# Block two's high weights meet both parts of the activations in one 512-column product, with the halves added outside TensorE

## What is computed

```python
h = concatenate([meta, x])                                   # 272 tokens
hn = rms_norm(h, norm_mix_g)
u, gb_in, gc_in, v_in, ga_lin, gbr_lin = split(hn @ w_in)     # each 2048 wide
pooled = causal_multiscale_pool(u)                            # windows 2, 4, 8, 16, minus the token
y_a = einsum("blgc,gcd->blgd", pooled, pool_w) * pool_scale   # 4 groups of 512
y_b = (gb_in * causal_conv3(gc_in * v_in, conv_w)) @ conv_out_w
g_a, g_b = split(sigmoid(concatenate([ga_lin, gbr_lin]) + b_gate))
h = h + (g_a * y_a + g_b * y_b) @ w_o
hn = rms_norm(h, norm_ffn_g)
gate, up = split(hn @ w_gate_up)                              # 5632 wide each
h = h + (silu(gate) * up) @ w_down
out = rms_norm(h, norm_final_g)[:, N_META:]
```

## Time and profile before

| | us |
|---|---|
| three runs, median (lowest to highest) | 3471.76 (3467.4 to 3475.43) |
| the profiled execution: its own time | 3463.28 |
| its span, first to last instruction | 3462.0 |
| PE busy, PEld busy | 3311.9, 2870.4 |
| DVE busy, ACT busy, POOL busy | 1650.5, 1359.4, 172.5 |
| mean granted TensorE clock | 0.982 of 2.4 GHz |

### The profile page before, as it was taken

One profiled execution on the slowest core, in us unless ns is written; L12 is line 12 of the kernel. 1 busy time (PEld: TensorE's weight loads), 2 busy tenths in 40 slices (PEclk: granted clock), 3 DMA queues, 4 the chain that ended last, 5 costly groups with the idle time before them and its releaser, 6 DMA issues.

```text
span 3462.0 us, 52180 instructions
## 1 busy us (share of the span) xinstructions
PE 3311.9 (96%) x21982; PEld 2870.4 (83%) x21982; DVE 1650.5 (48%) x2678; ACT 1359.4 (39%) x2179; POOL 172.5 (5%) x252
## 2 busy tenths in 40 slices
PE   6799999988999989999799999999999999999998
PEld 1488888863458888887459999999999999999998
DVE  0422233374563363355575675555555645545444
ACT  1422232344442263333454443344444444444343
POOL 2000000001001101000101000000000000000000
PEclk9999999998999999999899999999999999999999
DMA  9533222226744254443436455555555555555554
GB/s 344 187 122 122 91 93 96 84 74 239 251 174 151 92 193 142 140 134 108 156 119 200 151 182 177 182 178 189 186 186 188 165 186 187 189 186 186 189 185 138
DMA packets 154314, 566.06 MB, mean 164 GB/s; under 512 B 17472, under 2 KB 19648, under 8 KB 152928
## 3 DMA queue, kind: packets, MB, share of 16 engines
q1 hardware_dynamic: 147648, 529.52, 45.7%
q0 software_dynamic: 6432, 33.20, 2.7%
HBM read 550.07 MB, written 12.58 MB: 163 GB/s over the span
## 4 chain that ended last, share of the span: by engine, by line
PE 88%; DMA 5%; DVE 3%; ACT 2%; issue 1%; POOL 0%; SPq 0%; DVEq 0%; ACTq 0%; POOLq 0%
PE ps L695 20%; PE ps L696 20%; PE ps L697 20%; PE ps L688 7%; PE ps L690 7%; PE ps L689 7%; DMA sb_raw<-in_stream 5%; PE ps L614 2%; PE ps L816 1%; PE ps L802 1%; PE ps L779 1%; PE ps L795 1%; PE ps L770 1%; DVE sb_wlo L1236 1%; PE ps L727 1%
## 5 line engine op out<-in xcount | busy, mean ns | idle before, releaser
L1236 DVE TENSOR_TENSOR sb_wlo<-sb_raw,sb_whi 128x1024 fp32r<-128x1024 f32 (+1 forms) x818 | 996.8, 1219 | 1355.0 <-ACT sb_whi L891 1354.5
L891 ACT ACTIVATE sb_whi<-sb_raw 128x1024 fp32r<-128x1024 f32 (+1 forms) x818 | 859.4, 1051 | 1141.9 <-PE ps L697 912.3
L695 PE MATMUL ps<-sb_hn_hi,sb_whi 128*128 128x256 f32 (+1 forms) x2944 | 832.3, 283 | 4.1 <-DVE sb_hn_lo L1301 4.1
L696 PE MATMUL ps<-sb_hn_lo,sb_whi 128*128 128x256 f32 (+1 forms) x2944 | 832.7, 283 | 0.0
L697 PE MATMUL ps<-sb_hn_hi,sb_wlo 128*128 128x256 f32 (+1 forms) x2944 | 831.4, 282 | 0.0
L695 PEld LDWEIGHTS ps<-sb_hn_hi,sb_whi 128*128 128x128 f32 x2944 | 556.2, 189 | 4.7 <-DVE sb_hn_lo L1301 4.5
L696 PEld LDWEIGHTS ps<-sb_hn_lo,sb_whi 128*128 128x128 f32 x2944 | 555.8, 189 | 0.0
L697 PEld LDWEIGHTS ps<-sb_hn_hi,sb_wlo 128*128 128x128 f32 x2944 | 555.7, 189 | 0.0
L690 PE MATMUL ps<-sb_whi,sb_lo 128*128 128x512 f32 (+1 forms) x968 | 374.3, 387 | 0.0
L695 PE MATMUL ps<-sb_hi,sb_whi 128*128 128x512 f32 (+1 forms) x1056 | 359.9, 341 | 14.8 <-DVE sb_lo L1284 14.8
L696 PE MATMUL ps<-sb_lo,sb_whi 128*128 128x512 f32 (+1 forms) x1056 | 357.7, 339 | 0.0
(11 more groups left out here) (259 smaller groups left out, 3959.3 us busy)
## 6 DMA issues: line engine op xcount, KB each, us to landing
sb_raw<-in_stream SPq DMA_DIRECT2D x992, 512.0 KB, 3.4
sb_raw<-in_stream SPq DMA_DIRECT2D x18, 384.0 KB, 3.1
sb_T<-in_x POOLq DMA_DIRECT2D x1, 4096.0 KB, 16.0
...
```

The source lines that it names most:

```text
L695: PE.matmul(o, whi[:, s, w], xh, start=k == 0, stop=False)
L696: PE.matmul(o, whi[:, s, w], xl, start=False, stop=False)
L891: AC.activation(whi[:, s, 0:width], raw[:, r, 0:width], ACT.Copy).then_inc(*hi.up((g.id, c)))
L1236: VE.tensor_tensor(wlo[:, s, 0:width], raw[:, r, 0:width], whi[:, s, 0:width].bitcast(F32), ALU.subtract).then_inc(*lo.up((g.id, c)))
```

## The change

- All groups of block two but u, gc and v (`PAIRED`): the high and the low part of the activations now lie in one tensor, and the high weights meet both in one matmul of 512 columns, high part in the bank's first half, low part in the second. The low weights still meet the high part in a matmul of 256 columns, on the first half.
- The two halves of a bank are added outside: ACT copies the second half to SBUF (`half`), DVE adds the first (`both_sums`); in ya, wo and down DVE takes both halves itself, by one more instruction for each.
- u, gc and v run on 258 to 272 columns instead of 272: the tokens that are read.
- kpe: the low part goes into the second copy of the 64 columns, so two matmuls instead of three; a matmul with a "fold" matrix adds the halves.
- The dummy Sqrt moves to the third group of wout, wo and down; the attention pace of layer 0 goes from 3, 3, 2, 0 to 4, 2, 2, 0 chunks; the last multiplications are cut into a part by the weights (`scaled_out`, done early) and four instructions of 1,024 columns, and the output goes out in four transfers.

```diff
-ADA_PACE = ([8, 0] + [3, 3, 2, 0] * 11, [8, 0] + [2, 2, 2, 2, 0, 0] * 3)
+ADA_PACE = ([8, 0] + [4, 2, 2, 0] * 11, [8, 0] + [2, 2, 2, 2, 0, 0] * 3)
...
+PAIRED = ("ya", "gb", "ga", "gbr", "mix", "wo", "ffn", "down")
...
-        mix.append(Group("u", None, g, DT, 512, span(512 * g), N2, "hn", 4, "w_in_2", "hn_mix" if g == 0 else None))
+        mix.append(Group("u", None, g, DT, 512, span(512 * g), L + WINDOWS[g], "hn", 4, "w_in_2", "hn_mix" if g == 0 else None))
...
-        mix.append(Group("gc", None, j, DT, 512, span(2 * D + 512 * j), N2, "hn", 1, "w_in_2"))
+        mix.append(Group("gc", None, j, DT, 512, span(2 * D + 512 * j), L + 2, "hn", 1, "w_in_2"))
...
-        mix.append(Group("v", None, j, DT, 512, span(3 * D + 512 * j), N2, "hn", 1, "w_in_2"))
+        mix.append(Group("v", None, j, DT, 512, span(3 * D + 512 * j), L + 2, "hn", 1, "w_in_2"))
...
+                if g.kind in ("wout", "wo", "down") and g.index == 2 and c == 0:
+                    self.add("sqrt_table")
...
-        pl.add("sqrt_table")
...
+    NX = sb("hn", [P, 2, DT, N2], F32R, hn_at)
+    NH, NL = NX[:, 0, :, :], NX[:, 1, :, :]
...
-            a = META if g.x == "latent" else 0
+            a = 0 if g.kind == "ffn" else N2 - g.n
...
+    def both_parts(g, k):
+
+        if g.x == "pooled":
+            k += 4 * g.index
+        v = {"hn": NX, "latent": NX, "pooled": PX, "mixed": PX, "conv": CX, "ffn": FX}[g.x]
+        a = META if g.x == "latent" else 0
+        return v[:, :, k, a:a + L]
...
-        SP.wait_ge(*v_ev.at("final"))
-        SP.dma_start(d["out"], RES[:, :, META:]).then_inc(*out_out.up("out"))
-        SP.wait_ge(*out_out.at("out"))
+        for j in range(4):
+            SP.wait_ge(*v_ev.at("final", j))
+            SP.dma_start(d["out"][:, 4 * j:4 * j + 4, :], SCALED[:, 4 * j:4 * j + 4, :]).then_inc(*out_out[j].up("out"))
+        for j in range(4):
+            SP.wait_ge(*out_out[j].at("out"))
...
+                if g.kind in PAIRED:
+                    both = both_parts(g, k)
+                    for t in range(4):
+                        w = slice(w0 + t * P, w0 + t * P + P)
+                        PE.matmul(PS[:, g.base + t, :], whi[:, s, w], both, start=k == 0, stop=False)
+                        mm = PE.matmul(PS[:, g.base + t, 0:L], wlo[:, s, w], xh, start=False, stop=k == g.kt - 1)
+                elif g.kind in X_KINDS:
...
+                        if g.kind == "kpe":
+                            PE.matmul(o, whi[:, s, w], xh, start=k == 0, stop=False)
+                            mm = PE.matmul(o, whi[:, s, w], xl, start=False, stop=k == g.kt - 1)
+                            continue
...
-                        mm = PE.transpose(PS[:, g.base, t * P:(t + 1) * P], SC[:, 7, t * P:(t + 1) * P], ident)
+                        mm = PE.matmul(PS[:, g.base, t * P:t * P + HD], SC[:, 7, t * P:(t + 1) * P], C("fold"), start=True,
+                                       stop=True)
...
+        def half(dst, g, p):
+            AC.activation(dst, PS[:, g.base + p, L:], ACT.Copy).then_inc(*a_ev.up(("half", g.id, p)))
...
             elif g.kind == "gb":
                 k = 4 * g.index + p
+                if k >= 2:
+                    AC.wait_ge(*v_ev.at("conv_y", k - 2))
+                half(T3[:, 2 + p % 2, 0:L], g, p)
                 AC.wait_ge(*v_ev.at("conv_y", k))
                 AC.activation(CHI[:, k, 0:L], T3[:, p % 2, 0:L], ACT.Copy).then_inc(*a_ev.up(("conv", k)))
...
                 k = 4 * g.index + p
-                if k >= 2:
-                    AC.wait_ge(*v_ev.at("gated", k - 2))
-                AC.activation(T3[:, 2 + p % 2, 0:L], PS[:, g.base + p, 0:L], ACT.Sigmoid,
-                              bias=Pm("b_gate", k)).then_inc(
-                    *a_ev.up(("ga", k), *([("free", gid)] if p == 3 else [])))
+                AC.wait_ge(*(v_ev.at("gated", k - 2) if k >= 2 else v_ev.at("conv_y", DT - 2 + k)))
+                half(T3[:, 2 + p % 2, 0:L], g, p)
+                AC.wait_ge(*v_ev.at("ga_sum", k))
+                AC.activation(T3[:, 2 + p % 2, 0:L], T3[:, 2 + p % 2, 0:L], ACT.Sigmoid, bias=Pm("b_gate", k)).then_inc(
...
-                    AC.wait_ge(*v_ev.at("ffn_y", f - 2))
-                AC.activation(T3[:, 2 + p, 0:L], PS[:, g.base + p, 0:L], ACT.Silu).then_inc(
-                    *a_ev.up(("silu", f), *([("free", gid)] if p == 1 else [])))
+                    AC.wait_ge(*v_ev.at("ffn", f - 2))
+                half(T3[:, 2 + p, 0:L], g, p)
+                half(T3[:, p, 0:L], g, 2 + p)
+                AC.wait_ge(*v_ev.at("gate", f))
+                AC.activation(T3[:, 2 + p, 0:L], T3[:, 2 + p, 0:L], ACT.Silu).then_inc(*a_ev.up(("silu", f)))
...
+            if g.kind == "kpe":
+                v = whi[:, s, 0:width].rearrange("p (a b) -> p a b", b=P)[:, :, HD:P]
+                w_ = raw[:, r, 0:width].rearrange("p (a b) -> p a b", b=P)[:, :, HD:P]
+                VE.tensor_tensor(v, w_, v.bitcast(F32), ALU.subtract).then_inc(*lo.up((g.id, c)))
+                return
...
+        def scaled_out(k):
+            VE.tensor_scalar(SCALED[:, k, :], RES[:, k, META:], Pm("norm_final", k), None, ALU.mult).then_inc(*v_ev.up())
+
+        def both_sums(dst, g, p, *keys):
+
+            VE.wait_ge(*a_ev.at("half", g.id, p))
+            VE.tensor_tensor(dst, dst, PS[:, g.base + p, 0:L], ALU.add).then_inc(*v_ev.up(*keys))
...
-                VE.tensor_tensor(RES[:, k, META:], RES[:, k, META:], PS[:, g.base + p, 0:L], ALU.add).then_inc(
+                VE.tensor_tensor(RES[:, k, META:], RES[:, k, META:], PS[:, g.base + p, 0:L], ALU.add).then_inc(*v_ev.up())
+                VE.wait_ge(*v_ev.last())
+                VE.tensor_tensor(RES[:, k, META:], RES[:, k, META:], PS[:, g.base + p, L:], ALU.add).then_inc(
                     *v_ev.up(("x", g.kind, k), *([("free", gid)] if p == 3 else [])))
+                if g.kind == "down" and k < DT - 4:
+                    VE.wait_ge(*v_ev.last())
+                    scaled_out(k)
...
-                    VE.tensor_tensor(T2[:, dst, 16:16 + N2], T2[:, src, 16:16 + N2], T2[:, src, 16 - step:16 + N2 - step],
-                                     ALU.add).then_inc(*v_ev.up())
+                    a, b = 16 + N2 - g.n + 2 * step - 1, 16 + N2
+                    VE.tensor_tensor(T2[:, dst, a:b], T2[:, src, a:b], T2[:, src, a - step:b - step], ALU.add).then_inc(
+                        *v_ev.up())
...
-                    ins = VE.tensor_scalar(YA[:, k, 0:L], PS[:, g.base + m, 0:L], Pm("pool_scale", k), None, ALU.mult)
+                    VE.tensor_scalar(YA[:, k, 0:L], PS[:, g.base + m, 0:L], Pm("pool_scale", k), None, ALU.mult).then_inc(
+                        *v_ev.up())
+                VE.wait_ge(*v_ev.last())
+                for m in range(4):
+                    k = 4 * g.index + m
+                    ins = VE.scalar_tensor_tensor(YA[:, k, 0:L], PS[:, g.base + m, L:], Pm("pool_scale", k), YA[:, k, 0:L],
+                                                  ALU.mult, ALU.add)
                 ins.then_inc(*v_ev.up(("ya", g.index), ("free", gid)))
...
+                both_sums(T3[:, 2 + p % 2, 0:L], g, p)
                 VE.wait_ge(*v_ev.last())
-                VE.tensor_tensor(Y, Y, PS[:, g.base + p, 0:L], ALU.mult).then_inc(
+                VE.tensor_tensor(Y, Y, T3[:, 2 + p % 2, 0:L], ALU.mult).then_inc(
                     *v_ev.up(("conv_y", k), *([("free", gid), ("conv_read", g.index)] if p == 3 else [])))
...
-                VE.tensor_tensor(Y, PS[:, g.base + p, 0:L], G4[:, p, 0:L], ALU.mult).then_inc(
+                both_sums(Y, g, p)
+                VE.wait_ge(*v_ev.last())
+                VE.tensor_tensor(Y, Y, G4[:, p, 0:L], ALU.mult).then_inc(
...
-                VE.wait_ge(*a_ev.at("silu", f))
                 if f >= 2:
                     VE.wait_ge(*v_ev.at("ffn", f - 2))
-                VE.tensor_tensor(Y, T3[:, 2 + p, 0:L], PS[:, g.base + 2 + p, 0:L], ALU.mult).then_inc(
-                    *v_ev.up(("ffn_y", f), *([("free", gid)] if p == 1 else [])))
+                both_sums(T3[:, 2 + p, 0:L], g, p, ("gate", f))
+                both_sums(Y, g, 2 + p, *([("free", gid)] if p == 1 else []))
+                VE.wait_ge(*a_ev.at("silu", f))
+                VE.wait_ge(*v_ev.last())
+                VE.tensor_tensor(Y, T3[:, 2 + p, 0:L], Y, ALU.mult).then_inc(*v_ev.up(("ffn_y", f)))
...
+                VE.wait_ge(*v_ev.at("x", "down", DT - 1))
+                for k in range(DT - 4, DT):
+                    scaled_out(k)
+                VE.wait_ge(*v_ev.last())
                 rstd("down", T4[:, 1, :])
-                for k in range(DT):
-                    ins = VE.scalar_tensor_tensor(RES[:, k, META:], RES[:, k, META:], Pm("norm_final", k),
-                                                  T4[:, 1, 0:L], ALU.mult, ALU.mult)
-                ins.then_inc(*v_ev.up(("final",)))
+                for j in range(4):
+                    o = SCALED[:, 4 * j:4 * j + 4, :]
```

(2 more changed lines are left out.)

51 lines of the change are left out of this document (32 added, 19 removed).

## The result

The changed kernel takes 3450.36 us, median of 7 runs (3445.2 to 3459.25), beside 3471.76 us for the kernel before in its 7 runs (3467.4 to 3476.03). The ratio is 0.994, 95% interval 0.9927 to 0.9953: faster by 21.4 us, where 47.6 were forecast, and 2.4 us beyond the slow end of the range. The profiled execution's own time is 3450.92 us, its span 3449.6.

A forecast was written before the change was run, and what follows sets the result against it. Block two was taken as paced by how fast TensorE starts matmuls; -32.8 - 12.7 - 7.3 - 6.0 + 4.8 + 5.6 + 0.8 = -47.6 us gave 3424.2 us, range 3405 to 3448 us.

The forecast's parts named there:

- The joined product: Block two: a 512-column plus a 256-column step replace three of 256, saving 9.5 ns per trio, -32.8 us.
- Rival 1: Block two: the seam between two runs makes the joined step 232.5 ns, saving only 8.6 us; 3448.4 us, chance 0.09.
- Rivals 2, 3 and 4: In order: ffn evacuation waits, 3446 us, 0.08; joined step 248.3 ns, 3503 us, 0.04; narrow step 113 ns, 3409 us, 0.10.
- rival 3: Joined operand's second run: seam adds 13.3 ns, step 248.3 ns, decided from 241.3 on; 3503 us, chance 0.04.
- Narrower groups: Block two's gc, v, u1 and u2: fewer columns shorten each matmul, 7.0 ns in gc and v; -12.7 us.
- kpe: 16 k-tiles in two layers lose one 512-column step each, the fold costing nothing new; -7.3 us.
- The end: Final multiplications and output: four wide instructions and overlapped transfers take 8.0 instead of 14.0 us; -6.0 us.
- ya: Ends of ya1 to ya3: four more DVE instructions make TensorE wait 1.6 us each; +4.8 us.
- gb: TensorE waits 1.2 us at the ends of gc1 to gc3 and 2.0 at ga0's; +5.6 us.
- the drift: In gb's self-paced chain each piece comes 0.30 (0.50) us later than the one before, the fourth 0.9 (1.5).
- Stage ends: Ends of wo and down: eight additions delay the last tile, a table load leaves the chain; +0.8 us.
- Attention pace: Layer 0's attention: with 4 and 2 chunks the slot ends as it did; 0 us.

The follow-up runs named there:

- kernel 2: Changed kernel with rows of 256 instead of 272 columns in pooled, conv and ffn's hidden values, still two runs; 3446.55 us, one run.
- kernel 1: Changed kernel with the joined operand as one run of 512 columns, except in gb, ga and gbr; 3452.85 us, ratio 0.9951.
- kernel 9: Changed kernel with both products 512 columns wide in ffn (operand two runs) and down (operand one run); 3686.11 us, one run.
- kernel 12: Changed kernel with one-run operand (except gb, ga, gbr) and, per chunk, eight joined products before its eight of 256 columns; 3454.04 us, one run.
- kernel 3: Changed kernel with nothing joined, three products of 256 columns everywhere, all other trims kept; 3448.43 us, ratio 0.9935.
- Kernel 4: Changed kernel with ya and gb back to three products and their old evacuations, the other six kinds joined; 3439.83 us, ratio 0.9914.
- Experiment 8: Kernel 4 with layer 0's attention pace back at 3, 3, 2, 0 chunks; 3438.1 us, ratio 0.9912.

## Why the prediction was wrong

**The joined product, -32.8 us: this step failed.** Measured by the terms, it gives -4.3 us in ffn with down and about -2 in the mix stage, -6.3 in sum. The prediction set the joined step at 225.5 ns, between 224.2 and 226.7, because nothing in the trace of before spoke against block one's step. It was 232.5. That row lacks three things. The prediction named the first, the two runs. It passed over the second, that the row's neighbours are all of its own width, and over the third, the spacing of the rows, which it had noted itself for the steps of 256.

What the runs show in its place: in the change the pair takes 350.8 ns wherever it stands, and the layout of the operand's rows goes with that. On rows of 256 instead of 272, with two runs (kernel 2) or laid out as a single run (kernel 1), the same pair takes either 353.3 or 346.7 ns, and the second is the prediction's own slow end. So neither the two runs nor the narrow neighbours, nor both together, must hold the joined step up: kernel 2's ya groups have both and reach 346.7. Where all steps are 512 wide, two runs on rows of 272 take 231.9 ns and the single run 226.7 (kernel 9); that is nearly all of the 5.8 ns by which the change's joined step is over 226.7, but whether it is the seam or the spacing isn't separated. With a single run in rows of eight, a turn of the width costs some 20 ns (kernel 12). The cause stays open: nothing here shows what makes the pair 353.3 in one stretch and 346.7 in the next, nor why rows of 272 give 350.8. What is shown is that the form "two runs, rows of 272, narrow neighbours" steps at 232.5, and that no way of laying it out that was tried holds 346.7 over a stage.

**Rival 1** had the price right: it named 232.5 ns, and 3448.4 us against 3450.4; that the total comes so close is in part luck, since the other terms' errors cancel. Its reason, the seam, is not shown: kernel 9 would bear it out, kernel 2's ya groups speak against it. The rule that it quoted (the Trainium skill, "TensorE: Matmul & The Clock Gate", "Back-to-back issue gap") comes to the same sum, but no step is as it says: by it a 512-column step takes 215.8 ns, and the trace has 226.7 at best. The section gives that formula for a matmul by itself, and for a stream of weight loads and matmuls about 131 ns at 512 columns, which no stretch here shows either. Rivals 2, 3 and 4 did not happen: ffn has no wait for evacuations, the joined step is 8.8 ns below where rival 3 decides, and the narrow neighbour takes 118.3 ns, not 113. The case that came had a chance of 0.09, too little for a term of 33 us that rested on a form no row showed: the range's ends, -20 and -41, both assumed that this form would step like its nearest row.

**Narrower groups, -12.7 us: about right.** The mix stage with nothing joined (kernel 3) is 765.5 - 754.1 = 11.4 us shorter than before. In the change's timeline the 258-column steps of v0 lie 120.0 ns apart (44 starts, 43 steps in 5.16 us), 1.5 more than the 118.5 put; over all of gc and v the step is 119.5.

```profile
2068.76 0.28 PE L720 MATMUL ps<-sb_hn,sb_wlo 128*128 128x258 f32 x1
...
2073.92 0.28 PE L718 MATMUL ps<-sb_hn,sb_whi 128*128 128x258 f32 x1
```

**kpe, -7.3 us: right for the products, but the fold isn't free.** z with kpe takes 183.2 us instead of 186.9 in layer 0 and 114.4 instead of 118.0 in layer 1. The prediction said that the fold takes the place of four transposes at no cost; it is eight matmuls, and from the last projection before it to the first behind it there are 1.04 us instead of 0.59 in layer 0, and 1.03 instead of 0.59 in layer 1. That leaves -6.4.

**The end, -6.0 us: right.** 14.0 us have become 7.8: -6.2.

**ya, +4.8 us: right**, in place and size: three waits of 1.6, 4.9 us in all, made by four instructions of 1.66 us where 1.8 had been put. **gb, +5.6 us: right in place, too large.** Three waits of 0.7 on average and one of 1.2 make 3.4 us, where 3 x 1.2 + 2.0 stood; the drift was put too high. Kernel 4 confirms both, 8.2 us for 8.3. The 0.4 us at the end of wo0 wasn't foreseen.

**Stage ends, +0.8 us: too small.** From the last matmul of wo to the first of ffn there are 9.01 us instead of 8.14, and from the last of down to the last matmul of the rstd rows 6.63 instead of 5.57: +1.9 in sum. With nothing joined they are 7.44 and 4.57.

**The sum by what was measured:** -6.3 - 11.4 - 6.4 - 6.2 + 4.9 + 3.4 + 0.4 + 1.9 = -19.7 us, against the medians' -21.4. The two profiled executions differ by only 12.4, since the changed one spent 4.2 us more before the first projection, 4.2 more in layer 0's attention and 1.0 more between the layers, and 2.2 less in layer 1's attention. Experiment 8 shows the second to be scatter. The first varies in the same way from profile to profile: the last modulation matmul of the start comes between 116.7 and 122.9 us in the experiments, none of which edits the start.

**Attention pace, 0: right** (experiment 8).

So the chance of 0.93 for faster was borne out, by the trims; the joined product alone is 26.5 us off, as much as the whole forecast (26.2), and the errors of the other terms nearly cancel.
